# New distances in memory between the weight ring and the rows of a two-block transformer kernel, and x with the first weights in one transfer

## The reference

```python
h = h + 0.5 * swiglu(rmsnorm(h, g1), w_gate, w_up, w_down)      # FFN, 1024 -> 2816 -> 1024
z = rmsnorm(h, g) @ w_in                                        # 2464 + 3072 columns
y = stack(mla_mixer(z), diff_mixer(z), pool_mixer(z))           # three branches of 512 columns
h = h + sum(sigmoid(gates) * (y @ w_branch)) @ w_out
h = h + 0.5 * swiglu(rmsnorm(h, g2), v_gate, v_up, v_down)      # a second FFN
```

## Time and profile before

| | us |
|---|---|
| three runs, lowest / median / highest | 1486.43 / 1486.9 / 1487.59 |
| the profiled execution, its own time | 1486.53 |
| its span in the profile | 1484.7 |
| TensorE busy / VectorE / ScalarE | 1474.0 / 1160.1 / 793.5 |

### The profile page before, as it was taken

One profiled execution on the slowest core, in us unless ns is written; L12 is line 12 of the kernel. 1 busy time (PEld: TensorE's weight loads), 2 busy tenths in 40 slices (PEclk: granted clock), 3 DMA queues, 4 the chain that ended last, 5 costly groups with the idle time before them and its releaser, 6 DMA issues.

```text
span 1484.7 us, 23067 instructions
## 1 busy us (share of the span) xinstructions
PE 1474.0 (99%) x9684; PEld 1313.2 (88%) x9684; DVE 1160.1 (78%) x1534; ACT 793.5 (53%) x995; POOL 39.4 (3%) x41
## 2 busy tenths in 40 slices
PE   9999999999999999999999999999999999999999
PEld 8888898888988888888889878799999999989978
DVE  7987777687798875988758677879998899766844
ACT  6444455565454444544436566455545745775653
POOL 0000001210000000000001020000000000000000
PEclk9999999999999999999999999999999999999999
DMA  7555545434455545555553544455554453435531
GB/s 288 201 197 199 173 171 185 160 142 169 161 195 195 191 178 198 186 189 193 186 202 139 190 152 160 150 214 208 197 200 172 165 181 139 142 107 192 174 138 58
DMA packets 38967, 261.15 MB, mean 176 GB/s; under 512 B 4688, under 2 KB 5584, under 8 KB 9168
## 3 DMA queue, kind: packets, MB, share of 16 engines
q1 hardware_dynamic: 38000, 258.62, 49.0%
q10 hardware_dynamic: 864, 1.05, 0.2%
HBM read 258.61 MB, written 1.05 MB: 175 GB/s over the span
## 4 chain that ended last, share of the span: by engine, by line
PE 91%; DVE 7%; ACT 1%; issue 1%; DMA 0%; ACTq 0%
PE ps L291 20%; PE ps L228 13%; PE ps L230 13%; PE ps L229 13%; PE ps L298 10%; PE ps L781 8%; PE ps L786 4%; DVE w_low L213 3%; PE ps L316 1%; PE ps L1526 1%; PE ps L318 1%; DVE scratch L2229 1%; PE ps L1517 0%; DMA w_raw<-in_weights 0%; PE ps L1499 0%
## 5 line engine op out<-in xcount | busy, mean ns | idle before, releaser
L213 DVE TENSOR_TENSOR w_low<-w_raw,w_high 128x2048 fp32r<-128x2048 f32 (+2 forms) x244 | 551.4, 2261 | 151.8 <-ACT w_high L207 150.0
L207 ACT ACTIVATE w_high<-w_raw 128x2048 fp32r<-128x2048 f32 (+2 forms) x244 | 459.9, 1886 | 374.2 <-PE ps L298 167.7
L291 PE MATMUL ps<-x,w_high 128*128 128x512 f32 x1328 | 317.7, 391 | 0.0
L291 PEld LDWEIGHTS ps<-x,w_high 128*128 128x128 f32 x1328 | 243.3, 188 | 47.7
L298 PEld LDWEIGHTS ps<-x,w_low 128*128 128x128 f32 x1328 | 167.1, 188 | 7.0
L298 PE MATMUL ps<-x,w_low 128*128 128x256 f32 x1328 | 169.2, 280 | 0.0
L228 PE MATMUL ps<-w_high,x 128*128 128x512 f32 (+1 forms) x448 | 165.6, 370 | 0.0
L230 PE MATMUL ps<-w_high,x 128*128 128x512 f32 (+1 forms) x448 | 161.0, 359 | 0.0
L229 PE MATMUL ps<-w_low,x 128*128 128x512 f32 (+1 forms) x448 | 160.7, 359 | 0.0
L228 PE MATMUL ps<-x,w_high 128*128 128x256 f32 x456 | 130.1, 285 | 0.3 <-DVE x L354 0.3
L781 PE MATMUL ps<-ffn_hid,w_high 128*128 128x512 f32 x528 | 128.0, 392 | 0.0
(11 more groups left out here) (476 smaller groups left out, 2336.4 us busy)
## 6 DMA issues: line engine op xcount, KB each, us to landing
w_raw<-in_weights SPq DMA_DIRECT2D x231, 1024.0 KB, 4.9
w_raw<-in_weights SPq DMA_DIRECT2D x10, 768.0 KB, 4.5
w_raw<-in_weights SPq DMA_DIRECT2D x5, 512.0 KB, 3.8
even_second_vectors<-in_second SPq DMA_DIRECT2D x1, 1836.0 KB, 7.2
resid<-in_x SPq DMA_DIRECT2D x3, 256.0 KB, 6.5
w_raw<-in_weights ACTq DMA_DIRECT2D x3, 256.0 KB, 7.6
out<-resid SPq DMA_DIRECT2D x3, 256.0 KB, 2.3
table<-in_table SPq DMA_DIRECT2D x1, 737.0 KB, 8.2
```

Source lines behind the costliest of these rows:

```text
L207: act.activation(self.slot(self.wh, n), self.slot(self.raw, n), ACT.Copy).then_inc(self.hi_made, 1)
L213: dve.tensor_tensor(self.slot(self.wl, n), self.slot(self.raw, n), self.slot(self.wh, n).bitcast(F32), ALU.subtract).then_inc(self.lo_made, 1)
L291: pe.matmul(c.bank(bank + i).rearrange("p (a t) -> p a t", a=2), wh[:, k, i * P:(i + 1) * P], c.x[:, :, k, :], start=(k == 0), stop=False, ...
```

## The change

- The offsets of all slots are given by the distance between weights and rows, `below(rows)` = (8 - rows/4) mod 128 floats: `rows` is how many bytes the rows lie behind the weights. Slot 0 of every FFN stage stays at distance 0 in both rings, and so does the low part of slot 1 of the first.
- FFN stages (high, low): 16 and -64; 64 and -32; -64 and 48; 48 and -48. The down slots of the last: -64 in both rings.
- Mixers (slots formerly at 32 / formerly at 0): -64 and 16; -80 and 64.
- Even layer: -64, but 64 for q and k and 48 for v. Odd layer: -96 for `G_R`, -48 for q and k, -64 for v and z, 64 for the output.
- x and slot 0's weights are a second input, `first`, laid out by row tiles with x and weights side by side (2048 bytes a partition and tile). SyncE sends it in five pieces into a new tensor `setup_first`, then slot 1, slots 2 to 4 and the tables with no wait between, and last x once more into the residual `c.h` (1 MB). ScalarE sends the gains alone. The first stage's norm, high and low parts read the new tensor. VectorE waits for the residual's transfer before its first residual add.
- WARM goes from 18 to 9.

```diff
--- before.py
+++ after.py
@@ -25,7 +25,7 @@
 RING = 3
 FIRST_TILES = ((0, 1), (1, 2), (2, 4), (4, 6), (6, 8))
 PIECES = len(FIRST_TILES)
-WARM = 18
+WARM = 9
 EARLY_SLOTS = 5
 FC = 2 * P
 FF_STEPS = D_FF // FC
@@ -78,16 +78,34 @@
 SIZES = (([SLOT] * FF_SLOTS + [MIX_SIZE.get(n, SLOT) for n in range(MIX_SLOTS)] + [SLOT] * FF_SLOTS) * DEPTH
          + [EVEN_OUT if n >= A_OUT else SLOT for n in range(EVEN_SLOTS)]
          + [DT * P if n == G_R else SLOT for n in range(ODD_SLOTS)])
+LAST_DOWN = FF_SLOTS - 1
 LINE, ROOM = 8, 128
-FF_LOW = [LINE] + [0] * (FF_SLOTS - 1)
-LAST_DOWN = FF_SLOTS - 1
-LAST_HIGH = [0 if n in (*range(4, LAST_DOWN, 3), LAST_DOWN) else LINE for n in range(FF_SLOTS)]
-MIX_PHASES = [LINE if S_DV <= n < S_POOL or S_GATE <= n < S_OUT else 0 for n in range(MIX_SLOTS)]
-EVEN_PHASES = [LINE if A_V <= n < A_GLU else 0 for n in range(EVEN_SLOTS)]
-ODD_PHASES = [LINE if G_V <= n < G_OUT else 0 for n in range(ODD_SLOTS)]
-REST = EVEN_PHASES + ODD_PHASES
-HIGH_AT = ([LINE] * FF_SLOTS + MIX_PHASES + [LINE] * FF_SLOTS) * (DEPTH - 1) + [LINE] * FF_SLOTS + MIX_PHASES + LAST_HIGH + REST
-LOW_AT = (FF_LOW + MIX_PHASES + FF_LOW) * DEPTH + REST
+
+
+def below(rows):
+
+    return (LINE - rows // 4) % ROOM
+
+
+DOWN = (*range(4, LAST_DOWN, 3), LAST_DOWN)
+
+
+def ffn_at(high, low):
+    return [LINE] + [below(high)] * (FF_SLOTS - 1), [LINE] + [below(low)] * (FF_SLOTS - 1)
+
+
+def mixer_at(three, full):
+    return [below(full if S_DV <= n < S_POOL or S_GATE <= n < S_OUT else three) for n in range(MIX_SLOTS)]
+
+
+FFNS = [ffn_at(16, -64), ffn_at(64, -32), ffn_at(-64, 48), ffn_at(48, -48)]
+MIXERS = [mixer_at(-64, 16), mixer_at(-80, 64)]
+EVEN_AT = [below(-64 if n < A_Q or n >= A_GLU else 64 if n < A_V else 48) for n in range(EVEN_SLOTS)]
+ODD_AT = [below(-96 if n < G_Q else -48 if n < G_V else -64 if n < G_OUT else 64) for n in range(ODD_SLOTS)]
+LAST_HIGH = [below(-64) if n in DOWN else FFNS[3][0][n] for n in range(FF_SLOTS)]
+LAST_LOW = [below(-64) if n in DOWN else FFNS[3][1][n] for n in range(FF_SLOTS)]
+HIGH_AT = FFNS[0][0] + MIXERS[0] + FFNS[1][0] + FFNS[2][0] + MIXERS[1] + LAST_HIGH + EVEN_AT + ODD_AT
+LOW_AT = FFNS[0][1] + MIXERS[0] + FFNS[1][1] + FFNS[2][1] + MIXERS[1] + LAST_LOW + EVEN_AT + ODD_AT
 LOW_AT[1] = LINE
 N_SLOTS = len(SIZES)
 LAYER_SLOTS = 2 * FF_SLOTS + MIX_SLOTS
@@ -135,7 +153,7 @@
             self.sem(s) for s in ("resid_done", "sq_made", "sum_made", "mean_made", "root_made", "rstd_made"))
         self.xh_made, self.xl_made, self.column_made = self.sem("xh_made"), self.sem("xl_made"), self.sem("column_made")
         self.dve_chain, self.pool_chain, self.act_chain = (self.sem(s) for s in ("dve_chain", "pool_chain", "act_chain"))
-        self.vec_in = self.sem("vec_in")
+        self.vec_in, self.resid_in = self.sem("vec_in"), self.sem("resid_in")
         self.links = {"dve": 0, "pool": 0, "act": 0}
 
     def sem(self, name):
@@ -406,6 +424,10 @@
 
 
     LEFT = (0, 1, 4, 5)
+
+    def square(self, act, b):
+        c = self.c
+        act.activation(c.sq[:, 2 * b:2 * b + 2, :], self.rows[:, 2 * b:2 * b + 2, :], ACT.Square).then_inc(c.sq_made, 1)
 
     def add(self, dve):
         sq = self.c.sq
@@ -740,6 +762,8 @@
                 dve.wait_ge(*self.pair_done(p))
                 take_wide(c, dve, b.gate[:, :, :], B_DOWN + 2 * (p % 2)).then_inc(b.down_read, 1)
                 dve.wait_ge(*self.down_read(p + 1))
+                if base == 0 and p == 0:
+                    dve.wait_ge(c.resid_in, 16)
                 dve.scalar_tensor_tensor(out=h, in0=b.gate[:, :, :], scalar=0.5, in1=h, op0=ALU.mult,
                                          op1=ALU.add).then_inc(c.resid_done, 1)
                 self.next.low(dve, p)
@@ -845,35 +869,39 @@
 class Setup(Nothing):
 
 
-    def __init__(self, c, ctx, x, table, pos, vectors):
-        self.c, self.x, self.table, self.pos, self.vectors, self.norm = c, x, table, pos, vectors, None
+    def __init__(self, c, ctx, x, first, table, pos, vectors):
+        self.c, self.x, self.first, self.table, self.pos, self.vectors, self.norm = c, x, first, table, pos, vectors, None
         sb = lambda n, shape, dt=F32: ctx.enter_context(c.nc.sbuf_tensor(f"setup_{n}", shape, dt))
         self.pos_i, self.pos_f = sb("pos_i", [P, SEQ], I32), sb("pos_f", [P, SEQ])
         self.posq_i, self.posq_f = sb("posq_i", [P, 2], I32), sb("posq_f", [P, 2])
         self.ang, self.turns, self.dist_n = sb("ang", [P, SEQ]), sb("turns", [P, SEQ]), sb("neg_dist", [P, 3 * P])
+        self.room = sb("first", [P, DT, 2, SEQ])
+        self.rows, self.weights = self.room[:, :, 0, :], self.room[:, :, 1, :]
         self.piece_in = [c.sem(f"piece_in{b}") for b in range(PIECES)]
         self.half_in, self.tables_in, self.angle_made, self.sines_made, self.ones_made = (
             c.sem(s) for s in ("half_in", "tables_in", "angle_made", "sines_made", "ones_made"))
 
     def arrived(self, b):
-        return self.piece_in[b], 32 if b else 48
+        return self.piece_in[b], 16 if b else 32
 
     def piece(self, t, b):
-        first, end = FIRST_TILES[b]
-        return self.c.slot(t, 0)[:, first * FC:end * FC]
+        return self.c.slot(t, 0).rearrange("p (k n) -> p k n", k=DT)[:, slice(*FIRST_TILES[b]), :]
+
+    def weight_piece(self, b):
+        return self.weights[:, slice(*FIRST_TILES[b]), :]
 
     def high(self, act, b):
         c = self.c
         act.wait_ge(*self.arrived(b))
         for k in range(*FIRST_TILES[b]):
-            ins = act.activation(c.xh[:, k, :], c.h[:, k, :], ACT.Copy, scale=self.norm.gain[:, k:k + 1])
+            ins = act.activation(c.xh[:, k, :], self.rows[:, k, :], ACT.Copy, scale=self.norm.gain[:, k:k + 1])
         ins.then_inc(c.xh_made, 1)
 
     def low(self, dve, b):
         c = self.c
         dve.wait_ge(c.xh_made, b + 1)
         for k in range(*FIRST_TILES[b]):
-            ins = dve.scalar_tensor_tensor(out=c.xl[:, k, :], in0=c.h[:, k, :], scalar=self.norm.gain[:, k:k + 1],
+            ins = dve.scalar_tensor_tensor(out=c.xl[:, k, :], in0=self.rows[:, k, :], scalar=self.norm.gain[:, k:k + 1],
                                            in1=c.xh[:, k, :].bitcast(F32), op0=ALU.mult, op1=ALU.subtract)
         ins.then_inc(c.xl_made, 1)
 
@@ -883,11 +911,9 @@
     def sync(self, sp):
         c = self.c
         for b, (first, end) in enumerate(FIRST_TILES):
-            sp.dma_start(c.h[:, first:end, :], self.x[:, first:end, :]).then_inc(self.piece_in[b], 16)
-        sp.wait_ge(*self.arrived(0))
+            sp.dma_start(self.room[:, first:end], self.first[:, first:end]).then_inc(self.piece_in[b], 16)
         for b, s in enumerate((self.half_in, c.landed[1])):
             sp.dma_start(self.half(c.raw, b), c.weights[1][:, b * SLOT // 2:(b + 1) * SLOT // 2]).then_inc(s, 16)
-        sp.wait_ge(*self.arrived(2))
         for n in range(2, EARLY_SLOTS):
             c.load(sp, n)
         sp.dma_start(c.vec[:, DT:], self.vectors[:, DT:]).then_inc(c.vec_in, 16)
@@ -895,6 +921,7 @@
         with c.nc.allow_non_contiguous_dma(reason="256 positions, one a partition"):
             sp.dma_start(self.posq_i[:, :], self.pos.rearrange("o (a p) -> p (o a)", p=P)).then_inc(self.tables_in, 16)
         sp.dma_start(c.tab[:, :], self.table).then_inc(self.tables_in, 16)
+        sp.dma_start(c.h[:, :, :], self.x).then_inc(c.resid_in, 16)
 
     def gpsimd(self, pool):
         c = self.c
@@ -906,13 +933,11 @@
     def first_scalar(self, act):
         c = self.c
         act.dma_start(c.vec[:, 0:DT], self.vectors[:, 0:DT]).then_inc(self.piece_in[0], 16)
-        for b, (first, end) in enumerate(FIRST_TILES):
-            act.dma_start(self.piece(c.raw, b), c.weights[0][:, first * FC:end * FC]).then_inc(self.piece_in[b], 16)
         act.preload_act_table(ACT.Sqrt)
         act.wait_ge(self.ones_made, 1)
         for b in range(PIECES):
             self.high(act, b)
-            act.activation(self.piece(c.wh, b), self.piece(c.raw, b), ACT.Copy).then_inc(c.hi_made, 1)
+            act.activation(self.piece(c.wh, b), self.weight_piece(b), ACT.Copy).then_inc(c.hi_made, 1)
         for b, s in enumerate((self.half_in, c.landed[1])):
             self.norm.square(act, b)
             act.wait_ge(s, 16)
@@ -934,7 +959,7 @@
         for b in range(PIECES):
             self.low(dve, b)
             dve.wait_ge(c.hi_made, b + 1)
-            dve.tensor_tensor(self.piece(c.wl, b), self.piece(c.raw, b), self.piece(c.wh, b).bitcast(F32),
+            dve.tensor_tensor(self.piece(c.wl, b), self.weight_piece(b), self.piece(c.wh, b).bitcast(F32),
                               ALU.subtract).then_inc(c.lo_made, 1)
         for b in range(2):
             dve.wait_ge(c.hi_made, PIECES + 1 + b)
@@ -2524,7 +2549,7 @@
             sem(s) for s in ("kt_turned", "kt_copied", "scored", "masked", "ds", "st", "st_next"))
         self.o_made, self.o_rt, self.o_inverse, self.o_n, self.o_turned, self.o_z, self.o_high, self.o_low = (
```

(12 more changed lines are left out.)

## The result

The changed kernel takes **1493.8 us** (median of 4 runs, 1493.0 to 1495.0) where the kernel before takes 1486.8 (4 runs, 1486.4 to 1487.6): ratio 1.0043, 95% interval 1.0031 to 1.0055. It is 7.0 us slower; 1494.5 was forecast. The profiled execution took 1492.99 us with a span of 1491.2, 6.5 more than before's 1486.5 and 1484.7. The total is close, but it came out of other terms than the forecast's, which is luck in the sum, so the parts matter more here than the total.

The account below looks back on a forecast made before the run. TensorE's start-to-start matmul steps were taken to bound the kernel. 512-column steps +7.7, 256-column steps 0, -0.5 and +3.1, and the start -2.2 made +8.1 us on 1486.5, with 0.4 to the median: 1494.5 us, range 1471 to 1511.

Parts of the forecast that it names:

- Rival (a): All stages: distance does nothing to TensorE's steps and only the start's saving is left, 1484.3 us; chance 0.15.
- Part 1: 512-column matmuls in all stages: 1696 at multiples of 64 bytes unchanged, 1424 at other distances dearer; +7.7 us.
- if 64 bytes repeat, nothing changes: FFN 2 and 3, mixer 2, odd's v and z: 1696 512-column matmuls keep their step; 0 us.
- the 1424 others at 234, +7.7 us: FFN 1 and 4, mixer 1, even's values: 512-column steps rise from 228.6 to 234 ns; ends 0 and 7.7.
- Part 2: 256-column matmuls: 0 for 2560 at multiples of 64, -0.5 us for even's 384, +3.1 us for 2200 others.
- Rival (b): 256-column steps lock at half of 226.7 ns: 1467 us for all, 1475 with multiples of 64 alone; chance 0.25.
- -0.5 for even's q and k: Even layer's 384 256-column matmuls with rows standing: step goes from 118.2 to 116.8 ns, -0.5 us.
- +3.1 for the other 2200: 256-column matmuls not at multiples of 64: steps 1.4 ns dearer, at 118.2; +3.1 us, ends -7.5 and +7.0.
- Part 3: Kernel start: piece 2 lands at 6.6 instead of 8.78 us, -2.2 us at the end; ends 0 and -2.9.
- Warm-up at "cost 0": Kernel start: the shorter warm-up costs nothing, as first products end where piece 1 is awaited anyway; ends 0 and +1.
- Signs named ahead: Trace signs: FFN 1 and 4 some 234 ns, FFN 2 and 3 228 to 229, mixer 1 234, mixer 2 227.
- Rival (c): 512- and 256-column steps: nothing repeats at 64 bytes, only distance 0 is steady, every 512 pays; 1507 us, chance 0.25.

Follow-up runs that it names:

- dist_only: The changed kernel's distances with x, first weights and warm-up as in the kernel before: 1498.09 us, ratio 1.0065 to the kernel before.
- start_only: The changed start and its nine warm-up matmuls with all distances of the kernel before: 1486.27 us, ratio 0.9990 to the kernel before.
- swapped: The changed kernel with its 512-column distances moved to other stages or given the other sign: 1490.42 us, one run.
- best_held: best with 18 warm-up matmuls and the even layer's q and k back at distance 32: 1485.84 us, ratio 0.9991 to the kernel before.
- best: The changed kernel with all 512-column distances at 0 and all 256-column ones at -64: 1487.68 us, ratio 1.0002 to the kernel before.
- warm18: start_only with 18 warm-up matmuls instead of 9: 1485.53 us, ratio 0.9987 to the kernel before.

## Why the prediction came out right, and where it was wrong

The time was right, and the direction had its cause: distances make 512-column steps dearer, and the start gives back a little. That the sum came within 1 us is luck: the 512-column terms came out 2.4 us above the forecast and the 256-column ones 5.4 us below it.

- **That distance sets the step, and that the change is slower for it:** right. Rival (a), "the distance does nothing" (1484.3), fell. The Trainium skill (SBUF — State Buffer, Who interferes with whom) has TensorE's two read ports independent of each other; the trace does not bear out that addresses are then of no account: in FFN 3 the 512-column step goes from 228.9 to 233.0 ns in dist_only, which differs from the kernel before in the addresses of weights alone.
- **Part 1, "if 64 bytes repeat, nothing changes" for 1696 matmuls:** this is the step that failed. They cost 0.5 (FFN 2) + 2.0 (FFN 3) + 2.4 (mixer 2) + 0.2 (odd) = 5.1 us where the sum has 0. The ratio 226.7 = 17/16 of 213.3 on which the repeat was built says at most how much a step at distance 0 loses, not that other distances count by 64 bytes.
- **Part 1, the 1424 others at 234, +7.7 us:** mis-sized, +5.0. FFN 1 at 16 is free (228.7), FFN 4 at 48 is at 232.0; mixer 1 at -16 is above the upper bound, 235.9 against 234. One bound was used for both signs and both arrangements.
- Both together 10.1 against 7.7: of the 5.1 us that the repeat wrongly left out, FFN 1 (0.0 where 2.8 was forecast) and FFN 4 (1.1 for 1.8) gave back 3.5, and mixer 1 (3.6 for 2.6) took 1.0 more. The sum does not vouch for its terms.
- **Part 2, 0 for the 2560 at multiples of 64:** -3.7 measured, almost all of it at -64 in mixer 1 (-1.7) and the last down projection (-1.6), where whole stretches are at 113.3. Rival (b) was right for these stretches and wrong as a rule: even's 720 at the same -64 average 116.6. Rival (b)'s times, 1467 and 1475, also leave out Part 1's +7.7 that its own condition counts. **-0.5 for even's q and k:** -1.3, hidden by VectorE, a cover that the forecast did not price. **+3.1 for the other 2200:** +2.2.
- **Part 3, -2.2 us:** 1.6 in the trace and 2.1 in start_only's (first full group at 19.40 us); by the medians 1.4 alone (0.1 to 2.8 by the interval) and 2.1 with 18 warm-up matmuls. So the size was about right. Piece 2 came at 7.09, not at 6.6, and the reason given for 6.6 was wrong: by 7.1 us the windows of the changed kernel have some 1.6 MB moved (259 GB/s from 2 to 4 us, 357 to 6, 303 to 8), so the bytes were not late, but only 1 MB of them was pieces 0 to 2. The transfers queued behind ran beside piece 2, where the sum gave it the whole rate. Warm-up at "cost 0": the first products do start earlier (5.64 us instead of 7.95), but the nine matmuls end at 5.3, and TensorE then waits 2.35 us for piece 2's low half, longer than the 1.75 us of the kernel before.
- **The residual's DMA and wait, 0:** right. The residual add starts at 148.7 us, against 150.5 before, and no wait of VectorE there is for a DMA.
- Signs named ahead: FFN 1 and 4 at 234, mixer 2 at 227 and FFN 2 and 3 alike were wrong, mixer 1 dear and tokens below 118 right; and two signs named against the forecast were there: steps near 113.4 in a long run, and 512-column steps above 236 (236.3 in mixer 1). Rival (c), no repeat, every distance pays (1507), was right in its mechanism for 512 columns and over in its price: FFN 1 and FFN 2, a third of such steps, pay 1 ns or less.

Left open: why the sign matters, what picks 113.3 or 117.8, and why the odd layer's q and k at -48 take 120.5 ns in swapped and 117.7 in the changed kernel.

## What to carry to other kernels

Where TensorE's steps bound a kernel, the addresses of its two operands are a term worth up to 8 ns in 230: measure the signed distance in each arrangement before you move a tensor, and never carry a value from one sign, width or stage to another. When a start feeds TensorE earlier, fill the wait that it leaves: with 18 warm-up matmuls instead of nine the wait was 0.6 instead of 2.0 us, the clock was at its full level in all 11 runs instead of 6 of 11, and the gain was 2.1 instead of 1.4 us, though the intervals of the two overlap, and best_held with the same 18 was below the full clock in 5 of 11 runs. A forecast whose sum is right can still be wrong in every large term, so read the change stage by stage.

## What the runs showed of the hardware that was not expected

- With equal distance in size, the sign decides: 512 columns at +64 take 229.3 to 229.7 ns, at -64 232.8 to 233.4, in six stages and both arrangements.
- A long row of 256-column matmuls at -64 has two steady steps, 113.3 and 117.8 ns; two kernels with the same instructions up to there were in different ones over the same projection. In the FFNs it goes with the distance of the 512-column groups between: 117.8 with these at 0, 113.7 at -64, by turns at 16. At +32 the means of the FFN and mixer stages repeat from kernel to kernel within 0.1 ns (116.8).
- The granted clock fell to its lower level of 1.2 GHz behind waits of TensorE of 2.51 and 2.24 us (best) and of 1.88 us (dist_only), and stayed at 2.4 GHz behind waits of 2.74 and 2.23 us (swapped), 2.35 (the changed kernel) and 2.03 (start_only), one execution each. 10 of 11 runs of best have a mean clock below 1, and none of the 11 of warm18, whose profiled run has no wait over 1.0 us once the products have begun. The kernel before, whose profiled run has none over 1.8, has a mean clock below 1 in 11 of 21 runs.
- Faster matmuls can gain nothing: in the even layer they lengthen TensorE's longest wait for VectorE, from 1.1 us before to 1.9 in the changed kernel and 2.2 in best.
